# Hybrid conv/S5/MoE block on one core: token and vector loads on ScalarE's queue, finer first pieces, a later sum of squares, a shorter router

## What is computed

```
h  = rms_norm(x) * norm_mix                 # norm over the 1024 columns of each token
p  = h @ w_in                               # -> conv x | conv B | conv C | ssm u (512) | gate a | gate b
ya = (B * causal_conv3(C * x_conv)) @ w_conv_out
yb = glu(gelu(S5 scan of u))                # 32 groups, 64 complex states each
x  = x + (sigmoid(ga) * ya + sigmoid(gb) * yb) @ w_o
h2 = rms_norm(x) * norm_ffn
group  = argmax(h2 @ w_route_group + b)     # 4 groups of 8 experts
expert = top 2 of the group's 8 logits      # weights: softmax products
x  = x + sum over the 2 experts of weight * (silu(h2 @ gate) * (h2 @ up)) @ down     # ff 512
out = rms_norm(x) * norm_final
```

## Time and profile before

| | |
|---|---|
| median of 3 runs | 685.4 us (684.43 to 685.62) |
| profiled execution | 684.13 us, its span 682.4 us |
| TensorE matmul busy | 532.1 us, 78% of the span |
| VectorE, ScalarE, POOL busy | 209.6, 68.8, 49.4 us |
| mean TensorE clock granted | 0.906 of full |
| DMA | 242.33 MB, mean 355 GB/s |

### The profile page before, as it was taken

The page is one execution under the profiler, slowest core; times in us unless marked ns, Lnnn a source line. Parts: engine busy times, 40 slices in busy tenths (PEclk is TensorE's granted clock), DMA queues, the critical chain, the costliest instruction groups (busy, mean ns, idle before and its releaser), DMA issues.

```text
span 682.4 us, 7657 instructions
## 1 busy us (share of the span) xinstructions
PE 532.1 (78%) x3295; PEld 323.8 (47%) x3295; DVE 209.6 (31%) x443; ACT 68.8 (10%) x141; POOL 49.4 (7%) x78
## 2 busy tenths in 40 slices
PE   8999999999999999897857583483576548249685
PEld 7888888888888565452242140140123114014242
DVE  5999997969513133010000000010000001000002
ACT  4010000002011132110100000010001000001003
POOL 5121111111200021000000000000000000000000
PEclk9999999999999999999869695797879669688999
DMA  8981804274079999999999999999999999999994
GB/s 334 421 367 40 330 1 144 104 278 174 42 315 424 374 335 379 461 435 431 431 428 427 427 430 434 438 434 434 434 430 434 430 434 442 434 442 417 411 426 197
DMA packets 13118, 242.33 MB, mean 355 GB/s; under 512 B 1697, under 2 KB 2081, under 8 KB 5794
## 3 DMA queue, kind: packets, MB, share of 16 engines
q1 hardware_dynamic: 12656, 240.35, 83.8%
q10 hardware_dynamic: 434, 1.58, 0.6%
HBM read 240.88 MB, written 1.05 MB: 355 GB/s over the span
## 4 chain that ended last, share of the span: by engine, by line
DMA 49%; PE 47%; DVE 1%; SPq 1%; issue 0%; ACT 0%; POOL 0%; PEldq 0%; DVEq 0%
DMA all_slots<-in_middle 40%; PE bank L1364 28%; PE bank L1656 8%; DMA all_slots<-in_last_third 6%; PE bank L1483 4%; DMA all_slots<-in_mix 3%; PE bank L1701 2%; PE bank L1725 1%; PE bank L1353 1%; PE bank L1445 1%; PE bank L1458 1%; PE bank L1772 1%; PE bank L1507 0%; SPq L472 0%; PE bank L1735 0%
## 5 line engine op out<-in xcount | busy, mean ns | idle before, releaser
L1364 PE MATMUL bank<-all_slots 128*128 128x256 f32 x896 | 196.0, 380 | 0.4 <-DMA all_slots<-in_mix 0.4
L1364 PEld LDWEIGHTS bank<-all_slots 128*128 128x128 f32 x896 | 169.5, 190 | 26.4 <-issue 1.3
L1647 PE MATMUL bank<-all_slots,work_region 128*32 128x512 f32 x758 | 91.7, 633 | 60.4 <-DMA all_slots<-in_middle 59.0
L1656 PE MATMUL bank<-all_slots,work_region 128*32 128x512 f32 x384 | 56.1, 750 | 48.2 <-DMA all_slots<-in_middle 48.2
L1647 PEld LDWEIGHTS bank<-all_slots,work_region 128*32 128x32 f32 x758 | 24.9, 116 | 120.2 <-DMA all_slots<-in_middle 64.3
L1275 DVE TENSOR_TENSOR work_region<-work_region,bank 128x512 f32<-128x512 f32 x8 | 8.2, 1030 | 180.9 <-PE bank L1647 149.6
L1656 PEld LDWEIGHTS bank<-all_slots,work_region 128*32 128x32 f32 x384 | 13.9, 135 | 86.4 <-DMA all_slots<-in_middle 46.3
L1280 DVE COPY work_region<-bank 128x512 f32<-128x512 f32 x7 | 4.8, 692 | 124.6 <-PE bank L1656 109.0
L1599 PE MATMUL bank<-work_region,h_region 128*128 128x128 f32 x224 | 29.5, 288 | 8.5 <-issue 8.5
L1599 PEld LDWEIGHTS bank<-work_region,h_region 128*128 128x128 f32 x224 | 28.7, 205 | 12.2 <-issue 12.2
L1483 PE MATMUL bank<-all_slots,work_region 128*128 128x512 f32 (+2 forms) x80 | 29.2, 512 | 0.0
(11 more groups left out here) (229 smaller groups left out, 435.0 us busy)
## 6 DMA issues: line engine op xcount, KB each, us to landing
all_slots<-in_mix SPq DMA_DIRECT2D x16, 2048.0 KB, 10.2
all_slots<-in_first SPq DMA_DIRECT2D x9, 2048.0 KB, 15.5
all_slots<-in_middle SPq DMA_DIRECT2D x4, 1024.0 KB, 7.7
all_slots<-in_last_slices SPq DMA_DIRECT2D x1, 4096.0 KB, 40.2
all_slots<-in_last_slices SPq DMA_DIRECT2D x2, 2048.0 KB, 46.9
all_slots<-in_last_left SPq DMA_DIRECT2D x2, 2048.0 KB, 37.2
all_slots<-in_first SPq DMA_DIRECT2D x3, 768.0 KB, 7.1
all_slots<-in_mix SPq DMA_DIRECT2D x4, 512.0 KB, 6.9
```

Source lines behind the costliest of these rows:

```text
L1364: ins = MM(dst, w[:, k, n * P:(n + 1) * P], rhs[:, k, :], start=k == 0, stop=k == kn - 1)
L1647: ins = MM(bank[to][quarter(e), at:at + n], xT[:, k, quarter(e)], wt, start=k == 0, stop=k == KD - 1)
L1656: ins = MM(bank[2 + h][quarter(e), :], actT[:, c, quarter(e)], of_expert[e][:, D * c + 512 * h:D * c + 512 * h + 512], start=c == 0, stop= ...
```

## The change

The tokens (now five pieces: k = 0, k = 1, then three pairs) and the columns are issued by ScalarE, in the order tokens 0, columns, the other tokens; SP issues the u weights in six pieces (k = 0, k = 1, two pairs, k = 6, k = 7) and then the mixer units as before. The tokens of k = 0 and 1 are scaled by the gain on VectorE, ahead of its squares (semaphore `h_first_ready`), those of k = 2 to 7 on ScalarE as before. ScalarE takes a Sqrt of one column of the identity before its scaling, and the root of the mean ahead of the two Sin. The matmul of the sum of squares stands behind k = 6, not k = 3. The identity is multiplied four times before the projection, not seven. In the router the group number is stored already times 1e30 (`group_order`), so that one instruction subtracts and adds the expert logits where a mask and an addition did; the one-hot rows are compared with the places themselves, so that the conversion L1183 goes; `second_choices` follows. The wait for the slot numbers moves in front of `route(0)`. The diff is whole:

```diff
--- before.py
+++ after.py
@@ -31,6 +31,9 @@
 NEIGHBOURS = (RING, RING + 1, 3, 4, 5, 6, RING + 3, 0, 1, 2, MIX_RING, RING + 2)
 MIX_UNITS = 17
 U_PIECES = 4
+U_LANDS = ((0, 1), (1, 1), (2, 2), (4, 2), (6, 1), (7, 1))
+X_LANDS = ((0, 1), (1, 1), (2, 2), (4, 2), (6, 2))
+SCALED_FIRST = 2
 U_BANKS = (4, 5, 6, 7)
 SLOTS = 32
 PACK = P // SLOTS
@@ -152,7 +155,7 @@
         minus_one = sb("minus_one", [P, TB])
         br = sb("br", [P, NEG + NE])
         rs = sb("rs", [P, 16, TB])
-        from_end = sb("from_end", [P, NE])
+        group_order = sb("group_order", [P, NEG])
         slot_no = sb("slot_no", [P, SLOTS])
         slot_low = sb("slot_low", [P, SLOTS])
         top = sb("top", [P, TB, 8])
@@ -275,8 +278,9 @@
         sumsq = sem("sumsq")
         meansq = sem("meansq")
         rstd = sem("rstd")
-        x_cols_in = [sem(f"x_cols_in{i}") for i in range(U_PIECES)]
-        u_in = [sem(f"u_in{i}") for i in range(U_PIECES)]
+        x_cols_in = [sem(f"x_cols_in{k}") for k, _ in X_LANDS]
+        h_first_ready = sem("h_first_ready")
+        u_in = [sem(f"u_in{k}") for k, _ in U_LANDS]
         h_raw_ready = sem("h_raw_ready")
         square_step = sem("square_step")
         square_psum = sem("square_psum")
@@ -466,18 +470,9 @@
 
         @block.sync
         def _(sp):
-            sp.dma_start(cols[:], columns[:]).then_inc(cols_in, 16)
-
-            def first_piece(c):
-                sp.dma_start(w8(U_U)[:, 2 * c:2 * c + 2, :].rearrange("p k n -> p (k n)"),
-                             mix[U_U, :, 1024 * c:1024 * c + 1024]).then_inc(u_in[c], 16)
-
-            for c in range(U_PIECES):
-                sp.dma_start(x_raw[:, 2 * c:2 * c + 2, :].rearrange("p k t -> p (k t)"), x_columns[c]).then_inc(x_cols_in[c], 16)
-                if c == 0:
-                    first_piece(0)
-            for c in range(1, U_PIECES):
-                first_piece(c)
+            for i, (k, n) in enumerate(U_LANDS):
+                sp.dma_start(w8(U_U)[:, k:k + n, :].rearrange("p k n -> p (k n)"),
+                             mix[U_U, :, 512 * k:512 * k + 512 * n]).then_inc(u_in[i], 16)
             for u in range(1, MIX_UNITS):
                 if u == 4:
                     sp.dma_start(BT.rearrange("p b i n -> p (b i n)"), s5_b[:]).then_inc(b_in, 16)
@@ -687,8 +682,9 @@
 
             nc.gpsimd.affine_select(out=upper16[:], in_=ones[:], compare_op=ALU.is_gt, fill=0.0, base=0,
                                     pattern=[[1, P]], channel_multiplier=-1)
-            nc.gpsimd.iota(from_end[:], pattern=[[-1, NE]], base=NE, channel_multiplier=0,
-                           allow_small_or_imprecise_dtypes=True)
+            link(nc.gpsimd.iota(group_order[:], pattern=[[-1, NEG]], base=NEG, channel_multiplier=0,
+                                allow_small_or_imprecise_dtypes=True))
+            nc.gpsimd.tensor_scalar(group_order[:], group_order[:], -MASKED, None, ALU.mult)
             nc.gpsimd.iota(slot_no[:], pattern=[[1, SLOTS]], base=0, channel_multiplier=0,
                            allow_small_or_imprecise_dtypes=True)
             nc.gpsimd.iota(slot_low[:], pattern=[[1, SLOTS]], base=-int(UNSELECTED), channel_multiplier=0,
@@ -770,17 +766,26 @@
                 ins.then_inc(act_step, 1)
                 act.wait_ge(act_step, steps[0])
 
+            for i, (k, n) in enumerate(X_LANDS):
+                act.dma_start(x_raw[:, k:k + n, :].rearrange("p k t -> p (k t)"),
+                              x_columns[k // 2, :, T * (k % 2):T * (k % 2) + T * n]).then_inc(x_cols_in[i], 16)
+                if i == 0:
+                    act.dma_start(cols[:], columns[:]).then_inc(cols_in, 16)
+            act.wait_ge(consts, 1)
+            nc.scalar.activation(stat[:, 2:3], ident[:, 0:1], ACT.Sqrt)
             act.wait_ge(cols_in, 16)
-            for k in range(KD):
-                if k % 2 == 0:
-                    act.wait_ge(x_cols_in[k // 2], 16)
-                nc.scalar.activation(h_raw[:, k, :], x_raw[:, k, :], ACT.Copy,
-                                     scale=cols[:, R_GMIX + k:R_GMIX + k + 1]).then_inc(h_raw_ready, 1)
+            for i, (k0, n) in enumerate(X_LANDS):
+                if k0 < SCALED_FIRST:
+                    continue
+                act.wait_ge(x_cols_in[i], 16)
+                for k in range(k0, k0 + n):
+                    nc.scalar.activation(h_raw[:, k, :], x_raw[:, k, :], ACT.Copy,
+                                         scale=cols[:, R_GMIX + k:R_GMIX + k + 1]).then_inc(h_raw_ready, 1)
+            act.wait_ge(mean_ready, 1)
+            nc.scalar.activation(rstd_row, mean_row, ACT.Sqrt).then_inc(root_ready, 1)
             act.wait_ge(angle_ready, 1)
             nc.scalar.activation(s5c[:, 5, :], s5c[:, 4, :], ACT.Sin)
             nc.scalar.activation(s5c[:, 6, :], s5c[:, 4, :], ACT.Sin, scale=0.5).then_inc(sines_ready, 1)
-            act.wait_ge(mean_ready, 1)
-            nc.scalar.activation(rstd_row, mean_row, ACT.Sqrt).then_inc(root_ready, 1)
 
             def main(what, n):
                 if what == "x":
@@ -934,8 +939,14 @@
 
             V = nc.vector
 
+            dve.wait_ge(cols_in, 16)
+            for k in range(SCALED_FIRST):
+                dve.wait_ge(x_cols_in[k], 16)
+                V.tensor_scalar(h_raw[:, k, :], x_raw[:, k, :], cols[:, R_GMIX + k:R_GMIX + k + 1], None, ALU.mult)\
+                    .then_inc(h_first_ready, 1)
             for piece in range(U_PIECES):
-                dve.wait_ge(x_cols_in[piece], 16)
+                if piece >= 1:
+                    dve.wait_ge(x_cols_in[1 + piece], 16)
                 raw = x_raw[:, 2 * piece:2 * piece + 2, :].rearrange("p k t -> p (k t)")
                 V.tensor_tensor(squares[:, piece], raw, raw, ALU.mult).then_inc(square_step, 1)
                 if piece >= 1:
@@ -944,7 +955,6 @@
                         .then_inc(square_step, 1)
             dve.wait_ge(square_step, 2 * U_PIECES - 1)
             V.tensor_tensor(square_sum[:, 0:T], square_sum[:, 0:T], square_sum[:, T:2 * T], ALU.add).then_inc(square_step, 1)
-            dve.wait_ge(cols_in, 16)
             dve.wait_ge(dt_ready, 1)
             are, aim = cols[:, R_ARE:R_ARE + ST], cols[:, R_AIM:R_AIM + ST]
 
@@ -978,7 +988,8 @@
                 link(V.tensor_tensor(rstd_row, rstd_row, off, ALU.mult))
 
             def normed_tokens():
-                dve.wait_ge(h_raw_ready, KD)
+                dve.wait_ge(h_raw_ready, KD - SCALED_FIRST)
+                dve.wait_ge(h_first_ready, SCALED_FIRST)
                 for piece in range(U_PIECES):
                     V.tensor_tensor(hT[:, 2 * piece:2 * piece + 2, :], h_raw[:, 2 * piece:2 * piece + 2, :],
                                     rstd_row.unsqueeze(1).to_broadcast([P, 2, T]), ALU.mult).then_inc(hT_ready, 2)
@@ -1162,27 +1173,20 @@
                 def scalar(i):
                     return rs[:, i, b:b + 1]
 
-                def first_of(values, best, n, tmp):
-
-
-                    link(V.scalar_tensor_tensor(tmp, values, scalar(best), from_end[:, NE - n:], ALU.is_equal, ALU.mult))
-                    link(V.tensor_reduce(scalar(15), tmp, AX.X, ALU.max))
-
                 dve.wait_ge(rstd, 1 + b)
                 dve.wait_ge(logits_psum, b + 1)
                 link(V.scalar_tensor_tensor(lg[:, b, :], bank[LOGIT_BANKS[b]][:, 0:N_LOGITS], stat[:, 4 + b:5 + b], br[:],
                                             ALU.mult, ALU.add))
                 link(V.tensor_reduce(scalar(0), lg[:, b, 0:NEG], AX.X, ALU.max))
-                first_of(lg[:, b, 0:NEG], 0, NEG, group_first[:, b])
-                link(V.tensor_scalar(group_mask[:, b], group_first[:, b], scalar(15), MASKED, ALU.not_equal, ALU.mult))
-                link(V.tensor_tensor(in_group[:, b].rearrange("p (g e) -> p g e", g=NEG),
-                                     lg[:, b, NEG:].rearrange("p (g e) -> p g e", g=NEG),
-                                     group_mask[:, b].unsqueeze(2).to_broadcast([P, NEG, EG]), ALU.add))
+                link(V.scalar_tensor_tensor(group_first[:, b], lg[:, b, 0:NEG], scalar(0), group_order[:], ALU.is_equal, ALU.mult))
+                link(V.tensor_reduce(scalar(15), group_first[:, b], AX.X, ALU.max))
+                link(V.scalar_tensor_tensor(in_group[:, b].rearrange("p (g e) -> p g e", g=NEG),
+                                            group_first[:, b].unsqueeze(2).to_broadcast([P, NEG, EG]), scalar(15),
+                                            lg[:, b, NEG:].rearrange("p (g e) -> p g e", g=NEG), ALU.subtract, ALU.add))
                 link(V.max(out=top[:, b, :], in_=in_group[:, b]))
                 link(V.max_index(out=places[:, b, :], in_max=top[:, b, :], in_values=in_group[:, b]))
-                link(V.tensor_scalar(rs[:, 1:3, b], places[:, b, 0:2], -1.0, float(NE), ALU.mult, ALU.add))
-                link(V.tensor_scalar(first_hot[:, b], from_end[:], scalar(1), None, ALU.is_equal))
```

(21 more changed lines are left out.)

## The result

The changed kernel takes 691.35 us (median of 6, 690.71 to 693.77) against 685.41 (median of 6): +5.9 us on the medians. The ratio of the runs is 1.0092, interval 1.0075 to 1.0110, so 5.1 to 7.5 us slower. The forecast was 689.1, that is +3.7. The direction and the path were right, the size was 2.2 us short (5.9 against 3.7). The range was 686.0 to 691.5: the median lies at its edge, and the ratio applied to the time before gives 691.7, just past it.

A forecast was written before the change was run, and what follows sets the result against it. The bound was taken as TensorE in the mixer from 28.42 to 296 us, then expert-weight transfers. Late c0 +2.3, clock +1.6, router -0.2 gave +3.7 us: 689.1 on the median of 685.4, range 686.0 to 691.5.

The forecast's parts named there:

- What bounds it: TensorE in the mixer from 28.42 to 296 us, then expert-weight transfers; a TensorE delay there moves everything behind it.
- The mean's place: Sum-of-squares matmul behind k = 6: its 6.17 us chain is mostly uncovered, so TensorE stands 4.0 us before x0.
- that the squares come hardly later: Mean's input on VectorE: summed at 11.56 today, the two added scalings cost at most 2 x 0.42 us in front.
- The start: Start of the u projection, set by warm-up, first weights and first scaled tokens: taken 4.6 us, ends 3.6 and 6.3.
- Supply and clock under the projection: During the u projection, waiting for pieces and slow records after shorter warm-up: taken 0.9 us, bounds 0 and 2.5.
- The clock after the pause: TensorE behind the new pause before x0: granted clock falls, loss 1.6 us, bounds 0 and 2.25.
- a harmless pause: Rival: the pause before x0 leaves the clock unchanged, +2.1 us, 687.5; chance 0.22.
- SP's earlier issues: Mixer units issued about 1.5 us earlier from SP's queue; worth nothing since c0 is not ready before 30.7.
- The router: Two VectorE instructions go, 0.47 us in the second block; 0.2 us taken to reach the end, bounds 0 and 0.47.
- the second, the late start: Rival: first pieces land at 6.3 as now, x0 at 25.5 to 27.1, 690.5 to 692.5; chance 0.14.

The follow-up runs named there:

- first experiment: Changed kernel with the sum-of-squares matmul back behind k = 3, nothing else: 685.89 us, ratio to the kernel before 1.001.
- second: Kernel before with only the sum-of-squares matmul moved behind k = 6: 691.85 us, ratio 1.0101.
- sixth experiment: Changed kernel with all its pieces on SP's queue, columns first, tokens and weights alternating: 690.68 us, ratio 1.0099.
- seventh experiment: Changed kernel with twelve identity matmuls before the projection in place of four: 690.16 us, ratio 1.0085.
- fifth: Changed kernel with the columns issued first on ScalarE's queue, the tokens behind them: 692.49 us, ratio 1.0105.
- tenth experiment: Changed kernel with all pieces on SP's queue, sum-of-squares matmul behind k = 4, nine identity matmuls before the projection: 686.37 us, ratio 1.0023.
- ninth: Changed kernel with the sum-of-squares matmul behind k = 4 and twelve identity matmuls before the projection in place of four: 686.38 us, ratio 1.0024.
- fourth experiment: Kernel before with only the router part of the change, two VectorE instructions fewer per block: 684.99 us, ratio 0.9996.

## Where the prediction was right, and the step of it that failed

- **What bounds it.** Right. The delay of TensorE in the head came through whole: 5.63 us at x0, 6.76 at the last scan output, 6.6 at the end.
- **The mean's place.** Right, and the main cause: undone, 5.2 of 5.9 us come back (first experiment); alone, it costs 6.7 (second). The pause was forecast at 4.0 us and measured 3.95. One premise beside it was wrong without harm: that the squares come hardly later. They were summed at 15.27 in place of 11.56, because the tokens landed late. Behind k = 6 that costs nothing; behind k = 3 the matmul already waits for them (first experiment).
- **The start: this step failed.** I bounded the first landing by 3.6 and 6.3 and took 4.6, "near the columns' row because it is first in its queue". It was 6.54. The columns' 1.86 us had been measured at the head of a single queue with nothing ahead of them. On the second queue they took 4.8, and 4.2 even as the first there, and so both the step and its upper end failed: the 4.6 us of the 512 KB gave 0.80 + 4.6 = 5.4, and the 6.3 that I wrote is the start of the kernel before. That the projection starts at 4.57 on one queue (sixth experiment) does not bear the working out: there the landing of the first weights sets it, and the columns are not what it waits for. The error is +1.9 us.
- **Supply and clock under the projection: mis-sized.** Taken 0.9 between 0 and 2.5; the mean stood 20.36 - 6.54 - 12.08 = 1.74 us behind the full rate, an error of +0.8 us. With a warm start 1.0 of the 1.74 goes and 0.7 stays (seventh experiment). What stays is supply: ScalarE was to scale k = 2 from about 6, and did so from 10.35, when the tokens had landed.
- **The clock after the pause.** Taken 1.6, measured 1.7 (29.55 against 27.86). The 1.6 was a choice between 0 and 2.25, so that it hit this closely is in part luck. The clock fell in all five profiles with an unfilled pause (the changed kernel's and the second, fifth, sixth and seventh experiments') and in neither of the two with a filled one. The chance of 0.22 that I left to a harmless pause looks too large.
- **SP's earlier issues.** Worth nothing, as forecast; the mixer units were issued from 3.88 in place of 5.29. Once x0 is in time, c0 can go back to waiting for the third unit: it does in the tenth experiment, and does not in the ninth.
- **The router.** 0.41 us on VectorE as against 0.47 forecast; what reaches the end is not resolved.
- **The rivals.** It was the second, the late start, to which I had given 0.14: mean at 19.3 to 20.9 (20.36), x0 at 25.5 to 27.1 (26.62), 690.5 to 692.5 (691.35). Its times held (its "+4.5 to +6" is the delay of x0; at c0 it is 0.5 us less), its chance was too small: how a transfer fares beside another queue lay in no row that I had, and a bound that rests on a transfer at the head of an empty queue should have had less weight than the 4.6 us of the piece that stood among others.

The sum with the measured terms: 2.3 + 1.9 + 0.8 + 1.7 - 0.2 = 6.5, against a span that grew by 6.6. The -0.2 for the router is the one term that no run resolves. The medians grew by 5.9 only, since the profiled execution of the kernel before lay further under its median than that of the changed kernel. So the forecast of 3.7 was short by 2.2 us on the medians and by 2.9 on the spans.

## What to carry to other kernels

Before a small matmul that opens a long chain of dependent steps is moved back, add up the chain (here 6.2 us) and what covers it behind the new place (2.2): the difference is a pause, and a pause of 4 us on TensorE was followed here by three to four microseconds at half the clock, five times out of five. What is needed first should be issued in front of the large loads: the 58 KB of the columns took 4.8 us on a second queue beside a stream of weights, 1.86 in front of it. Compare versions of different sessions by how far each stands from the same kernel timed beside it: in the seventh experiment a difference of medians of 1.2 us is one of 0.7 that way. And a term priced from one execution may differ in the next: the kernel's first microseconds were fast in the execution I read and slow in another with the same warm-up.

## What the runs showed that I had not expected

- In every profile here the granted clock reads 1.00 from the start of the trace, while the records show half rate until the first rise (four 256-wide records a microsecond between 7 and 9 us in the changed kernel). There the count of records is the better gauge.
- Seven warm-up matmuls (3.2 us) did not always raise the clock before the projection: at full rate in the kernel before and in the fourth experiment, at half in the second. The rule of the Trainium skill that the prediction cited (TensorE: Matmul & The Clock Gate, Part 1: The HAM clock gate), that the count of slow matmuls differs from run to run, agrees with this. Nine (4.2 us) did not in the tenth, where the records ran at four a microsecond from 6 to 8 us; twelve did in all five versions that had them.
- The Trainium skill says that starting DMAs on several engines only saves the sequencer's time, since all run on the same engines (DMA: Bandwidth & Descriptors, Issuing engines are not separate DMA queues). Here there was a cost besides: 4.8 us against 1.9 for the columns, and with the same pieces, in another order, 6.54 against 4.57 for the first matmul.
- A fall of the clock behind a pause of 2.25 and 2.36 us near the end made the last matmuls slow in two of the fourteen profiles (fifth and ninth experiments; 3.78 in place of 1.98 us for four records): from last scan output to end 496.7 us there against 493.1 in the kernel before. The pause was long because a transfer landed late, which nothing in the edits touches; so I take it that any version can meet it, and it is larger than most of what was compared here.
- Such a fall costs nothing where transfers set the pace. In the changed kernel the clock also fell behind a pause of 2.55 us before 650.76, and 32 records took 5.34 us in place of 3.64; from last scan output to end it is 492.9 us all the same.
